# Hybrid Fourier and attention block: a new order of the projection's small steps, a halved last output tile, and a swapped pair of loads

## The reference, cut to what matters

```python
def reference(x, c, ctx, c_ctx, norm_g, w_mod, b_mod, w_in, q_g, k_g, w_f, w_o, final_g):
    cos, sin = axial_rope_tables(rows)
    for l in range(DEPTH):                                  # DEPTH = 1
        h = rmsnorm(x, norm_g[l]) * (1 + scale[:, None]) + shift[:, None]
        pc_kv = hc @ w_in[l][:, K0:GA0]                     # 256 context rows: k and v alone
        k_ctx = rmsnorm(split_heads(pc_kv[..., :KV_W], N_KV_HEADS), k_g[l])
        p = h @ w_in[l]                                     # 2048 x 1024 by 1024 x 2304
        q = apply_axial_rope(rmsnorm(split_heads(p[..., Q0:K0], N_Q_HEADS), q_g[l]), cos, sin)
        k = apply_axial_rope(rmsnorm(split_heads(p[..., K0:V0], N_KV_HEADS), k_g[l]), cos, sin)
        attn = blocked_gqa(q, concat(k, k_ctx), concat(v, v_ctx))      # 8 heads, 2 kv heads of 64
        y = concat(attn * silu(ga), fourier_mix(fu, w_f) * silu(gf)) @ w_o
        x = x + gate[:, None] * y
    return rmsnorm(x, final_g)
```

## Time and profile before

| | us |
|---|---|
| three timed runs | 1409.53, 1409.7, 1410.79 |
| median | 1409.7 |
| profiled execution, its own time | 1412.48 |
| its span, first to last instruction | 1410.7 |
| TensorE busy in the span | 1362.8 |
| DVE busy | 865.1 |
| ScalarE busy | 575.4 |
| Pool busy | 615.8 |

### The profile page before, as it was taken

How to read it: one execution, slowest core, us unless ns; L and a number is a source line. 1 busy time by engine, 2 the same in 40 slices (tenths; PEclk the granted TensorE clock), 3 DMA queues, 4 the chain that set the end, 5 groups by cost and what they waited for, 6 DMA issues and landing times.

```text
span 1410.7 us, 22314 instructions
## 1 busy us (share of the span) xinstructions
PE 1362.8 (97%) x7878; PEld 926.1 (66%) x7878; DVE 865.1 (61%) x1263; ACT 575.4 (41%) x1061; POOL 615.8 (44%) x309
## 2 busy tenths in 40 slices
PE   6888999999999999999999999999999999999997
PEld 4677785555555555555555554888887888778886
DVE  3677677778777777777777778412322721755452
ACT  3454334545555455545454547232322323522120
POOL 0334115988888889888888883100000000000000
PEclk9999999999999999999999999999999999999999
DMA  9656429011101110111010100922511151785651
GB/s 365 232 151 211 121 67 259 23 38 34 33 26 37 30 37 27 39 30 37 26 37 30 30 26 21 301 79 105 177 47 38 35 226 53 203 210 178 195 154 75
DMA packets 84341, 142.63 MB, mean 101 GB/s; under 512 B 7085, under 2 KB 54325, under 8 KB 83386
## 3 DMA queue, kind: packets, MB, share of 16 engines
q1 hardware_dynamic: 76890, 129.09, 29.0%
q0 software_dynamic: 6672, 12.58, 3.2%
q10 hardware_dynamic: 720, 0.15, 0.1%
HBM read 112.30 MB, written 29.50 MB: 101 GB/s over the span
## 4 chain that ended last, share of the span: by engine, by line
PE 85%; issue 2%; DMA 2%; DVE 1%; ACT 1%; SPq 1%; POOLq 0%; POOL 0%; DVEq 0%
PE pv_ps L1574 18%; PE ring_ps L1558 10%; PE ring_ps L1559 9%; PE acc L63 7%; PE acc L64 7%; PE acc L65 7%; PE ring_ps L1502 6%; PE o_ps L63 4%; PE o_ps L65 4%; PE o_ps L64 4%; PE q_ps L63 1%; PE ring_ps L1582 1%; DMA gin<-rest_scratch 1%; PE q_ps L64 1%; PE q_ps L65 1%
## 5 line engine op out<-in xcount | busy, mean ns | idle before, releaser
L1284 POOL TENSOR_TENSOR prob_sum<-prob_sum,prob 128x1024 f32<-128x1024 f32 x217 | 526.9, 2428 | 86.7 <-DVE prob_sum L1409 63.7
L1388 DVE TENSOR_REDUCE chunk_max<-ring_ps 128x1 f32<-128x512 f32 x496 | 307.7, 682 | 88.2 <-PE ring_ps L1502 87.0
L1323 ACT ACTIVATE prob<-ring_ps 128x512 f32<-128x512 f32 x576 | 290.5, 633 | 72.1 <-PE ring_ps L1559 71.9
L1574 PE MATMUL pv_ps<-prob,v 128*32 128x512 f32 x2304 | 262.1, 598 | 0.0
L1558 PE MATMUL ring_ps<-blk_q_hilo,k_hi 128*128 128x512 f32 x576 | 235.4, 409 | 3.9 <-ACT prob L1323 1.8
L1559 PE MATMUL ring_ps<-blk_q_negm,k_lo 68*128 68x512 f32 x576 | 228.8, 397 | 0.0
L1574 PEld LDWEIGHTS pv_ps<-prob,v 128*32 128x32 f32 x2304 | 68.4, 110 | 151.1 <-issue 135.3
L63 PE MATMUL acc<-hh,w_rest_hi 128*128 128x512 f32 x384 | 151.1, 394 | 0.5 <-DVE hl L98 0.5
L64 PE MATMUL acc<-hl,w_rest_hi 128*128 128x512 f32 x384 | 150.4, 392 | 0.0
L65 PE MATMUL acc<-hh,w_rest_lo 128*128 128x512 f32 x384 | 150.3, 391 | 0.0
L1558 PEld LDWEIGHTS ring_ps<-blk_q_hilo,k_hi 128*128 128x128 f32 x576 | 110.1, 191 | 53.0 <-DVE blk_q_negm L1170 13.8
(11 more groups left out here) (315 smaller groups left out, 1956.6 us busy)
## 6 DMA issues: line engine op xcount, KB each, us to landing
xt_raw<-in_xt SPq DMA_DIRECT2D x16, 512.0 KB, 5.2
x_tok<-in_x SPq DMA_DIRECT2D x16, 512.0 KB, 4.9
blk_q_max<-q_scratch SPq DMA_DIRECT2D x64, 128.0 KB, 2.6
blk_q_hilo<-q_scratch SPq DMA_DIRECT2D x32, 256.0 KB, 2.7
h_raw<-in_xg SPq DMA_DIRECT2D x4, 2048.0 KB, 9.2
rest_scratch<-stage SPq DMA_DIRECT2D x32, 256.0 KB, 2.3
gin<-rest_scratch SPq DMA_DIRECT2D x16, 512.0 KB, 10.8
x_res<-in_x SPq DMA_DIRECT2D x16, 512.0 KB, 3.4
```

The lines of the kernel that those rows point to most:

```text
L1284: nc.gpsimd.tensor_tensor(acc_pool[slot][:], acc_pool[slot][:], prob[j][:], ALU.add).then_inc(s_psum, 1)
L1323: nc.scalar.activation(prob[j][:, e * QB:(e + 1) * QB], score_bank(t)[:], ACT.Exp).then_inc(s_exp, 1)
L1388: nc.vector.reduce_max(chunk_max[:, q, c:c + 1], ring[banks[c]][:], X_AXIS).then_inc(s_mfree, 1)
L1574: last = nc.tensor.matmul(pv_ps[row:row + QUAD], k.v[:, 2 * j + e, kvh, half * QUAD:(half + 1) * QUAD], prob[j][:, e * QB:(e + 1) * QB], s ...
```

## The change

**Projection.** A new pair of tables sets the turns: turns 1, 2, 3, 4 and 6 move (turn 1 from the end of tile 4 to its middle, turn 2 from the middle of 5 to the end of 4, turn 3 from the end of 5 to its middle, turn 6 from the middle of 8 to the end of 7). DVE's low parts have three places instead of one: ahead of `x_low` (`SPLIT_FIRST`), ahead of the head norm (`SPLIT_MID`) and behind it (`SPLIT_END`). `deviation` moves ahead of `x_low` in even tiles, and for pair 5 from tile 8 to tile 7. On ScalarE the copies of `TURN_MID` stand ahead of `x_high`, tile 3's reads and `sd_copy` ahead of `x_high` and `x_squares`, and `x_high(10)` in tile 7. SyncE's stores have their own table, `STORE_AT`: 1 at tile 4, 2 and 3 at 5, 4 at 6, 5 at 7, 6 at 9, 7 at 10.

**Last q.** `q_products` holds the two products; tile 16's stand ahead of `max_rows`, tile 17's ahead of its sums.

**Output.** `load_group(1)` stands ahead of the first two loads of x. The last tile is added, squared, scaled and stored in two halves of 512 columns; the first half's sum goes into the mean by itself.

DVE in the projection, tile 4, before: rope of k, x low part of tile 6, context weights, deviation 3, then the head norm begins.

```diff
-TURN_MID = {5: (2,), 6: (4,), 7: (5,), 8: (6,), 10: (7,), 11: (9,)}
+TURN_MID = {4: (1,), 5: (3,), 6: (4,), 7: (5,), 10: (7,), 11: (9,)}
...
+STORE_AT = {3: (0,), 4: (1,), 5: (2, 3), 6: (4,), 7: (5,), 9: (6,), 10: (7,), 12: (10,)}
...
@@ SyncE, projection
-                for m in SPLIT_AFTER.get(n - 1, ()):
-                    if latent(m):
-                        store_q(m)
+                for m in STORE_AT.get(n, ()):
+                    store_q(m)
@@ ScalarE, projection
+            def late_reads(n):
                 if latent(n):
                     q_read(n)
                 for m in TURN_END.get(n, ()):
                     turned_high(m)
                 if n % 2 and n + 1 < NT:
                     sd_copy((n + 1) // 2)
+            for n in range(2, LAST[0]):
+                kv_read(n)
+                for m in TURN_MID.get(n, ()):
+                    turned_high(m)
+                if n == 3:
+                    late_reads(n)
+                if n + 2 < NT and n != 8:
+                    x_high(n + 2)
+                if n + 4 < NT:
+                    x_squares(n + 4)
+                if n == 7:
+                    x_high(n + 3)
+                if n in (4, 5):
+                    for c in range(4 * (n - 4), 4 * (n - 3)):
+                        ctx_high(c)
+                if n != 3:
+                    late_reads(n)
@@ DVE, projection
                 kv_rope(n)
+                if n % 2 == 0 and n not in (2, 8):
+                    deviation((n + 2) // 2)
+                for m in SPLIT_FIRST.get(n, ()):
+                    turned_low(m)
+                if n == 7:
+                    variance(5)
                 if n + 2 < NT:
                     x_low(n + 2)
...
-                if n % 2 and n + 3 < NT:
+                if n % 2 and n != 7 and n + 3 < NT:
                     variance((n + 3) // 2)
-                if n % 2 == 0 and n + 2 < NT:
-                    deviation((n + 2) // 2)
+                if n in (2, 7):
+                    deviation((n + 3) // 2)
+                for m in SPLIT_MID.get(n, ()):
+                    turned_low(m)
                 if n in MAXIMA0:
                     reduce_block0(n)
                 head_norm(n)
-                for m in SPLIT_AFTER.get(n, ()):
+                for m in SPLIT_END.get(n, ()):
                     turned_low(m)
...
             q_sums(LAST[0])
+            q_products(LAST[0])
             k.max_rows(dve, row_ps, 0, 0)
             q_norm(LAST[0])
+            q_products(LAST[1])
             q_sums(LAST[1])
             q_norm(LAST[1])
@@ SyncE, output
             sp.wait_ge(s_dft, RADIX * GROUPS)
+            load_group(1)
             for e in range(2):
                 sp.dma_start(x[e][:], x_v[e]).then_inc(s_x[e], 16)
-            load_group(1)
...
+            for n in range(2):
+                sp.wait_ge(s_out, TT + n)
+                sp.dma_start(out_v[TT - 1][:, HALVES[n]], res[1][:, HALVES[n]]).then_inc(s_ost[1], 16)
@@ ScalarE, output
+            nc.scalar.activation(square[:, 1, HALVES[0]], res[1][:, HALVES[0]], ACT.Square,
+                                 accum_out=part_stat).then_inc(s_sum, 1)
+            act.wait_ge(s_add, TT + 1)
+            nc.scalar.activation(square[:, 1, HALVES[1]], res[1][:, HALVES[1]], ACT.Square,
+                                 accum_out=stat[1]).then_inc(s_sum, 1)
@@ DVE, output
+            for n in range(2):
+                dve.wait_ge(s_o, TT + n)
+                nc.vector.tensor_tensor(res[1][:, HALVES[n]], o_ps[1][:, n, :], x[1][:, HALVES[n]],
+                                        ALU.add).then_inc(s_add, 1)
+                if n == 0:
+                    dve.wait_ge(s_sum, TT)
+                    nc.vector.tensor_scalar(mean[1], part_stat, 1.0 / D, EPS, ALU.mult, ALU.add).then_inc(s_mean, 1)
+            dve.wait_ge(s_sum, TT + 1)
+            dve.wait_ge(s_mean, TT)
+            nc.vector.scalar_tensor_tensor(mean[1], stat[1], 1.0 / D, mean[1], ALU.mult, ALU.add).then_inc(s_mean, 1)
+            dve.wait_ge(s_rstd, TT)
+            for n in range(2):
+                nc.vector.scalar_tensor_tensor(res[1][:, HALVES[n]], res[1][:, HALVES[n]], rstd[1],
+                                               k.final_bc[:, HALVES[n]], ALU.mult, ALU.mult).then_inc(s_out, 1)
@@ TensorE, output: the last tile's first half is signalled too
-                    last.then_inc(s_o, 1)
+                        if n or (g == N_OG - 1 and e):
+                            last.then_inc(s_o, 1)
```

More of the change, by code:

```diff
@@ L103 @@
 CTX_TILES = (8, 9)
-TURN_MID = {5: (2,), 6: (4,), 7: (5,), 8: (6,), 10: (7,), 11: (9,)}
-TURN_END = {3: (0,), 4: (1,), 5: (3,), 10: (8,), 11: (10,)}
-SPLIT_AFTER = {2: (0,), 3: (1, 2), 4: (3, 4), 6: (5,), 7: (6,), 9: (7,), 10: (8, 9), 11: (10,)}
+TURN_MID = {4: (1,), 5: (3,), 6: (4,), 7: (5,), 10: (7,), 11: (9,)}
+TURN_END = {3: (0,), 4: (2,), 7: (6,), 10: (8,), 11: (10,)}
+SPLIT_FIRST = {4: (2,)}
+SPLIT_MID = {3: (1,), 4: (3,), 5: (4,), 8: (6,), 10: (8,)}
+SPLIT_END = {2: (0,), 6: (5,), 9: (7,), 10: (9,), 11: (10,)}
+STORE_AT = {3: (0,), 4: (1,), 5: (2, 3), 6: (4,), 7: (5,), 9: (6,), 10: (7,), 12: (10,)}
 LAST = (NT - 2, NT - 1)
@@ L109 @@
     TURN_END[_n] = (_n - 1,)
-    SPLIT_AFTER[_n] = (_n - 1,)
-SPLIT_AFTER[LAST[0]] = (LAST[0] - 1,)
+    SPLIT_END[_n] = (_n - 1,)
+    STORE_AT[_n + 1] = (_n - 1,)
+STORE_AT[LAST[1]] = (LAST[0] - 1,)
 CHUNKS = SEQ // QB
@@ L561, in _ @@
             x_squares(5)
-            for n in range(2, LAST[0]):
-                kv_read(n)
-                if n + 2 < NT:
-                    x_high(n + 2)
-                if n + 4 < NT:
-                    x_squares(n + 4)
-                if n in (4, 5):
-                    for c in range(4 * (n - 4), 4 * (n - 3)):
-                        ctx_high(c)
-                for m in TURN_MID.get(n, ()):
-                    turned_high(m)
+            def late_reads(n):
                 if latent(n):
@@ L765, in q_sums, with q_products @@
                                         eps_var[n // 2 % 3][:, n % 2:n % 2 + 1], ALU.mult, ALU.add).then_inc(s_hmean, 1)
-            def q_norm(n):
+            def q_products(n):
                 t = q_index(n)
+                dve.wait_ge(s_qsq, t + 1)
                 dve.wait_ge(s_qp, t + 1)
@@ L774, in q_norm @@
                                         ALU.mult).then_inc(s_qmul, 1)
+            def q_norm(n):
+                t = q_index(n)
                 dve.wait_ge(s_qmul, t + 1)
@@ L1747, in tail @@
         minus_half = res_small[:, 6:7]
+        part_stat = res_small[:, 7:8]
+        HALVES = (slice(0, D // 2), slice(D // 2, D))
         ones = at("ones", AT_SMALL + 128, [P, P])
@@ L1889, in _ @@
                 e = t % 2
-                pool.wait_ge(s_mean, t + 1)
+                pool.wait_ge(s_mean, t + 1 if t < TT - 1 else TT + 1)
                 nc.gpsimd.tensor_tensor(rstd[e], mean[e], minus_half, ALU.pow).then_inc(s_rstd, 1)
@@ L2125, in _ @@
                         dve.wait_ge(s_ost[e], 16 * g)
+                    if t == TT - 1:
+                        break
                     nc.vector.tensor_tensor(res[e][:], o_ps[e][:].rearrange("p a n -> p (a n)"), x[e][:],
```

13 lines of the change are left out of this document (8 added, 5 removed).

## The result

The changed kernel takes 1395.17 us in the median of 4 runs (1394.52 to 1398.69), the kernel before 1409.62 us (4 runs, 1408.13 to 1410.79): 14.4 us less by the medians. The ratio is 0.9907, with a 95% interval of 0.9894 to 0.9921, which is 11.1 to 14.9 us. The forecast was 1390.4 in a range of 1386.5 to 1398: the direction and the range hold, and the gain is 4.8 us smaller than forecast. The measured time also lies above the narrower range that the forecast had for itself (1387.5 to 1393). The profiled execution took 1394.5 us for a span of 1392.7. That is 18.0 us less than the span of before, and so 3.6 us more than the medians give.

A forecast was written before the change was run, and what follows sets the result against it. TensorE's idle time was taken to bound the kernel, since attention and most of the output wait for it. Terms 13.6 + 0.9 + 3.6 + 1.2 = 19.3 us off the 1409.7 median gave 1390.4, range 1386.5 to 1398.

The forecast's parts named there:

- issue time only: Rival, output: the new load order gains only its earlier issue, 0.8 us in place of 3.6; 1393.2 us, chance 14%.
- the chain shifts: Rival, projection: turn 5's thin margin and DVE waiting for ScalarE's copies take back 6 to 7 us; 1397 us, chance 16%.
- turn 5: Projection, tile 7: head norm 5 ready at 105.0 against TensorE's 106.6, the thinnest margin, 1.6 us; the 1.9 wait goes.
- Change 1: Projection: reordered turns, copies, low parts, deviations and q stores gain 13.6 us (9.7 + 2.2 + 1.7), bounds 8 and 15.3.
- five of six gone: Projection: of TensorE's six waits, 13.1 us, five go and one of about 3 us stays at tile 10's close.
- the term of 9.7 for `sd_row` 5: Projection, close of tile 10: sd_row 5 ready at 127.0, 9.7 us earlier, with 1.3 us off the 15.3 us chain.
- the 1.7 us of slow clock at turn 9: Projection, tiles 10 and 11: the slow clock behind the 2.2 us wait for low part 8 goes, gaining 1.7 us.
- what is late next: Projection, tile 10: new x_low wait of 0.5 to 1.2 us, then some 3 us for sd_row 5 through SyncE's chain.
- Change 2: Last q: earlier rope products remove the 1.31 us wait for the sine product; gain 0.9 us, bounds 0.2 and 1.3.
- give back a part: Last q: ScalarE's exponentials follow back to back and return part of the removed wait, leaving 0.9 us.
- Change 3: Output: gates of group 1 loaded ahead of x gain 2.0 us of pause and 1.7 of slow clock, rounded to 3.6.
- Change 4: Output's end: halved last tile saves 0.54 in add, 0.46 in squares, 0.3 in store; 1.2 us, bounds 0.5 and 1.6.

The follow-up runs named there:

- the memset's: Loads-ahead kernel (changed kernel, SyncE's x loads before block 0's) with DVE's memset of k_lo's ones rows ahead of x low part 3: 1387.59 us against 1388.68.
- load order alone: Kernel before with only the gates of output group 1 loaded ahead of x: 1408.03 us, ratio 0.9993.
- halves alone: Kernel before with only the last output tile done in two halves: 1407.64 us, ratio 0.9991.
- last q alone: Kernel before with only the rope products of the last q moved ahead of its sums: 1409.07 us, ratio 0.9999.
- the kernel with the order undone: Changed kernel with SyncE's x loads ahead of block 0's, and x again loaded ahead of output group 1's gates: median 1389.58 us against 1388.68.
- sd_row, loads or all three ahead: Changed kernel with sd_row 5 ahead of ScalarE's x work: 1389.34 us; SyncE's x loads ahead of block 0's: 1388.15; both plus y low part ahead: 1388.10.

## Why the prediction was right, and where its size was not

The range held because it was made wide enough for the rivals. The measured 1395.2 lies between the times of two of them, "issue time only" (1393.2) and "the chain shifts" (1397), but turn 5 kept its margin, and the loads cost more than their issue where the pause came. So the place in the range is not the merit of a rival: it comes from terms taken from one execution.

**Change 1, sized 13.6.** Measured 12.2 by the medians of the change alone (9.2 to 14.4) and 12.3 in the pair of profiles. The order of the waits came out as chained: five of six gone, one left at the close of tile 10, none at the turns 3, 4, 5 and 9, and a wait of 0.75 for x low part 10 at 121.8. (Turn 4 stays in the middle of tile 6, as the prediction has it; the list of moved turns names it by mistake.) Turn 5's head norm ended at 106.27, TensorE came at 107.72: 1.4 us of margin where I had 1.6. Two things are off. The first is the term of 9.7 for `sd_row` 5, which came to 8.2: it was ready at 128.5, not 127.0. Low part 5 ended 0.9 later (the stage started 0.7 later, inside the 57.5 to 58.7 at which the fourth close starts over all profiles but the memset's), and the chain took 14.6, not 14.0. The x rows were used 5.6 us after their issue, which is 0.7 off the old 6.3 where I took 1.3 off. Behind that close the kernel gained 4.1 us where the sum had 3.9. Attention took nothing back: at full clock E is 995.6 with the new table alone and 995.6 with the old (load order alone).

The second is the 1.7 us of slow clock at turn 9, which I counted as a sure gain. All four profiles with the old table have the pause there (2.2, 2.2, 3.0 and 3.0 us), but only two have a granted clock below 0.99 in the 10 us behind it. Where the earlier trace rows have 0.66, halves alone (TensorE back at 149.1) and last q alone (back at 150.2) have 1.00:

```profile
150.00:155.00 5.00, 5.00 (x23) 4.09 (x23) 2.16 (x6) 0.00 (x0) 1.01 (x1) 1.00 0.06 25
150.00:155.00 5.00, 4.76 (x22) 4.01 (x23) 2.29 (x7) 0.39 (x1) 1.01 (x1) 1.00 0.26 107
```

Over the four profiles with the old table A varies from 220.8 to 225.7, over the three with the new and this wait from 211.6 to 213.5, and the means are 10.3 apart. The chain through SyncE that I named as what is late next was right: each of the two ways to shorten it took the wait away.

**Change 2, sized 0.9.** Measured 0.2 by the medians (interval 1.8 slower to 2.1 faster), and -0.3 on stretch B. The step that failed is "give back a part": ScalarE's exponentials and the maxima of block 1 give back all. With the slow clock in B something may be left: E without its last wait is 996.8 in the two such profiles with the old order and 996.2 to 996.4 in the five with the new. These are too few to call it shown. The removed wait was real, but what followed was not bound by it.

**Change 3, sized 3.6.** The step that failed is the one ahead of the sum: a pause of one execution was taken as a pause of each. Where it comes it costs 3.5 to 5.9 us (C of 181.9 to 184.3 against 178.4), so that the term was right there or too small. It does not come in one of five profiles with the old order, nor, by their times, in three of the five runs of the kernel with the order undone. The medians gave 1.3 and 0.9 us, the means of the second pair 2.5, some of which can be the slow clock in B (1.2 us in the one profile). The rival "issue time only, 0.8" has the size of the medians, but not the mechanism.

**Change 4, sized 1.2.** Measured 1.40 on stretch D (means of the ten profiles with halves and the four without). Add 0.69 and squares 0.63 are as sized (0.69, 0.60), the two scales 1.41 instead of 1.32; from the end of the last scale to the end of the span it is 2.5 us against 3.1 in before, 0.6 less where I had 0.3.

**Not foreseen.** TensorE waits 1.2 us for a low part of y at the start of the output (0.2 before), behind the gate of w_o, whose load was used 15.9 us after its issue, against 14.9 in before. The pair of profiles loses 1.0 us there; in the kernels with sd_row, loads or all three ahead the wait is not there, and with the memset early it is 0.5 us.

**The sum.** 12.2 + 0.2 + 1.3 + 1.4 to 1.7 is 15.1 to 15.4, against 14.4 measured together: the terms add within their intervals. I had subtracted 19.3, of which 5.3 were pauses and slow clock (3.6 before group 1, 1.7 at turn 9) that the profiled execution had. For both, other profiles of the same code show that they do not come each time. It stood 2.8 us above its median, and I wrote that down and carried the terms over unshrunk. That the excess lies just there is not shown; the other executions of before left no trace.

## What to carry to other kernels

When the profiled execution lies above the median, price each pause that hangs on the landing of a DMA by its margin over several executions, not by its length in one. A removed wait counts only if what comes behind it on the other engines is earlier too: compare the time from one fixed point to another far behind, at equal clock. Price a fall of the clock behind a pause as a chance too. A stall that stands behind two queues can be removed at either of them: look for the engine on which the wanted instruction only stands in the wrong place.
